# Hybrid attention, convolution and expert block on one core: four high-part buffers, full-width row operations, and one-hot masks built by two tokens

## Chip, cores and metric

The program runs on one core of one Trainium2 chip. The metric is device time in microseconds (us). Before the change three runs took 1897.51, 1898.70 and 1901.18 us, median 1898.7 us. The profile is of one further execution, which took 1894.76 us.

## What is computed

The input is 256 tokens of width 2048. A first half (adaLN modulation, differential attention, causal convolution, output projection) takes about a quarter of the time and is not touched except for the layout of its last product. The second half is an expert retrieval (PEER) over 128 x 128 experts, of which each token picks 16 for each of 8 heads:

```python
q = (h @ w_q).reshape(T, PEER_HEADS, PEER_KEY_DIM)
s1 = jnp.einsum('thd,kd->thk', qb[..., :half], k1)
s2 = jnp.einsum('thd,kd->thk', qb[..., half:], k2)
v1, i1 = lax.top_k(s1, PEER_TOPK)
v2, i2 = lax.top_k(s2, PEER_TOPK)
cand = v1[..., :, None] + v2[..., None, :]
top, pos = lax.top_k(cand, PEER_TOPK)
g = jax.nn.softmax(top)
act = jax.nn.gelu(jnp.einsum('thkd,td->thk', u_tab[idx], hb)) * g
return jnp.einsum('thk,thkd->td', act, v_tab[idx])
```

## The kernel before

**Two ways through the experts.** For 192 tokens (TD) the kernel computes the product with all 16384 rows of u densely, and later the product with all rows of v, with a routing matrix that is zero where an expert was not picked. For the last 64 tokens (TS) it gathers the picked rows: 64 gathers of 128 rows of u (one row of 2048 floats per partition), each turned into 128 dot products by DVE, and 64 gathers of v, each added to a sum by DVE.

**Units.** Weights come as 544 units of 128 x 1024 floats, two to a block of 1 MB, into a ring `raw` of eight units. To keep accuracy with the fast fp32r format each unit is split: ACT copies it to fp32r (the high part, `w_hi`, function `hi`), DVE subtracts to get the low part (`w_low`, function `lo`), and PE multiplies the high part with the activations' high and low parts (L887, 8 matmuls of 2 x 192 columns) and the low part with the high activations (L894, 8 matmuls of 192 columns). `w_hi` has two buffers: `hi` of unit s waits until PE (`hi_used`) and DVE (`lo_ready`) are done with unit s - 2.

**Stages.** WQ (32 units, all 256 tokens, L1093), then the dense product with u in three stages, UP (64 units), MID (64) and ROUTE (128), then the product with v, DOWN (256 units, L1235). A stage runs in iterations of 16 units; the first is written out, the others are a hardware loop. Within an iteration the units are numbered j = 0 to 15, and each engine has its own fixed order of work by unit:

- PE, `product`: for each block (units 2m and 2m + 1) high then low matmuls of each half. A block's low activations' share stands in another part of the PSUM bank; ACT copies it out (`put_low`, L708, after the block's last matmul), and PE adds it back with an identity matmul (`add_low`, L868). This stands at the start of the second half of the next block. Then ACT applies gelu (L716), which frees the bank for the block after the next.
- DVE in UP and MID: `lo` for each unit, between them the steps of the top-k chain (`experts`, two in 16 units). In MID and ROUTE also the dots of gathered rows (`dots_at`, L1314), each row in two halves of 1024 with a read of the accumulator behind each; MID has 4 rows in an iteration, ROUTE 6, DOWN 4 row sums (`add_row`, L1741), also in halves.
- ROUTE builds the routing matrix for 24 tokens in an iteration, in 6 groups of 4: DVE makes two one-hot masks for each token (`make_masks`: L1277 the first for four tokens at once, L1282 the second for each, scaled by the gate in the same instruction) in one buffer, PE multiplies them (`weights`, L1187, 4 matmuls fp32, two records each), ACT copies the result out (`put_weights`, L731). The tables MASK, USE and PUT say at which unit each engine does group g. The single buffer ties them: `make_masks(g)` waits for `weights(g - 1)`.
- ACT: for each unit `hi`, then `put_low` at odd and gelu at even units, then in ROUTE `put_weights` at the units of PUT.
- SP brings the weights, POOL gathers the rows: u rows into two buffers, v rows into four (`got`).

```python
USE, MASK, PUT = (1, 4, 6, 9, 12, 14), (0, 3, 5, 8, 11, 13), (3, 6, 8, 11, 14, 15)
DOTS_ROUTE_FIRST = DOTS_ROUTE = (0, 1, 3, 4, 5, 6, 8, 9, 11, 12, 13, 14)
act.wait_ge(hi_used, at(i, ph.per, s - 1))
act.wait_ge(lo_ready, at(i, ph.per, s - 1))
```

Of the kernel before, what the change touches and what calls it, by code (L numbers as in the profile page):

```python
# [92 lines left out]
SUMS_FIRST, SUMS_AT = (6, 8, 9, 10, 12, 13, 14, 15), (0, 2, 4, 6, 8, 10, 12, 14)  # L93
# [10 lines left out]
def build_block(nc, x, c, c_row, w_ada, w_gate_f, b_cols, g_cols, rows, w_front, lambdas, g_subln, conv_w,  # L104
                conv_vecs, peer_wq, peer_keys, peer_u, u_rows, peer_v, out):
    with ExitStack() as ctx:
# [88 lines left out]
        a_pair = a2[:, :].rearrange("p (k m t) -> p k m t", m=2, t=T)  # L195
        a_hi, a_lo = a_pair[:, :, 0, :], a_pair[:, :, 1, :]
# [1663 lines left out]
```

## Time and profile before

| | |
|---|---|
| median of three runs | 1898.7 us |
| profiled execution | 1894.76 us, span 1892.9 us |
| PE / PE weight load busy | 1796.9 us (95%) / 1564.3 us (83%) |
| DVE busy | 1605.2 us (85%) |
| ACT busy | 850.1 us (45%) |
| POOL busy | 181.2 us (10%) |
| HBM traffic | 617.98 MB, mean 326 GB/s |
| chain that ended last | PE 73%, DVE 13%, issue 7%, DMA 6% |

The chain follows the work that ended last back from the end; its longest piece is PE's L1235 (DOWN), 582.93 us. Busy shares are averages over stages that have different limits, so they say little of what a change in one stage is worth: a stage is read by its own windows and by the rows of one iteration.

### The profile page before, as it was taken

How to read it: one execution, taken by the hardware profiler on the slowest of the kernel's cores; microseconds unless marked ns; L12 is line 12 of the kernel's file. 1: busy time of each engine (PE TensorE's matmuls, PEld its weight loads, DVE VectorE, ACT ScalarE, POOL GpSimd, SP SyncE). 2: the span in 40 equal slices, each digit the busy share in tenths (PEclk: the TensorE clock that was granted, in tenths of full speed). 3: DMA queues.
4: the chain of work that ended last, by engine and by line, in shares of the span. 5: the costliest groups of instructions: out<-in, count | busy, mean ns of one | idle time of the engine just before them, and what ended most of it. 6: DMA issues, size and time to landing. Idle time of an engine off the chain costs nothing.

```text
span 1892.9 us, 29014 instructions
## 1 busy us (share of the span) xinstructions
PE 1796.9 (95%) x9902; PEld 1564.3 (83%) x9902; DVE 1605.2 (85%) x2621; ACT 850.1 (45%) x1208; POOL 181.2 (10%) x145
## 2 busy tenths in 40 slices
PE   4999999898899999888899999999999999999997
PEld 4888888443899999777899999997888888888885
DVE  3668898766677999999999999997988888888887
ACT  3001222300645555444456666665554555555544
POOL 1000000000000000100021221211111111111110
PEclk9999999999899999999999999999999999999999
DMA  8998556699596677977889999999999999999994
GB/s 344 418 421 334 224 222 225 256 392 422 206 346 246 225 246 248 341 284 282 290 295 362 362 362 364 351 365 351 396 363 371 369 363 375 365 365 373 366 383 183
DMA packets 96785, 617.98 MB, mean 326 GB/s; under 512 B 11697, under 2 KB 20433, under 8 KB 25041
## 3 DMA queue, kind: packets, MB, share of 16 engines
q1 hardware_dynamic: 66960, 465.60, 64.1%
q0 software_dynamic: 18496, 134.24, 18.7%
q10 hardware_dynamic: 11266, 17.32, 2.5%
q8 instruction: 38, 0.62, 0.1%
q14 instruction: 25, 0.20, 0.0%
HBM read 600.26 MB, written 16.79 MB: 326 GB/s over the span
## 4 chain that ended last, share of the span: by engine, by line
PE 73%; DVE 13%; issue 7%; DMA 6%; ACT 1%; DVEq 0%; ACTq 0%; SPq 0%
PE ps L1235 31%; PE ps L887 10%; PE ps L894 6%; PE ps L932 6%; PE ps L916 4%; PE ps L1093 4%; PE ps L1043 3%; PE ps L943 3%; DMA early<-in_w_front 2%; DVE w_low L1292 2%; PE ps L1187 2%; DVE big L1314 2%; DMA early<-in_w_ada 1%; DMA big<-in_w_gate_f 1%; DMA gsub<-in_g_subln 1%
## 5 line engine op out<-in xcount | busy, mean ns | idle before, releaser
L616 ACT ACTIVATE w_hi<-raw 128x1024 fp32r<-128x1024 f32 x544 | 577.0, 1061 | 638.9 <-PE ps L1235 245.1
L1292 DVE TENSOR_TENSOR w_low<-raw,w_hi 128x1024 fp32r<-128x1024 f32 x544 | 661.5, 1221 | 103.2 <-ACT w_hi L616 95.1
L887 PE MATMUL ps<-a,w_hi 128*128 128x384 f32 x2048 | 410.2, 341 | 4.9 <-ACT stage L716 4.0
L1235 PE MATMUL ps<-w_hi,a 128*128 128x512 f32 x1536 | 391.2, 390 | 3.8 <-DVE a L1715 3.8
L887 PEld LDWEIGHTS ps<-a,w_hi 128*128 128x128 f32 x2048 | 347.6, 189 | 5.9 <-ACT stage L716 4.1
L1235 PEld LDWEIGHTS ps<-w_hi,a 128*128 128x128 f32 x1536 | 288.9, 188 | 64.3 <-issue 4.0
L894 PEld LDWEIGHTS ps<-a,w_low 128*128 128x128 f32 x2048 | 261.7, 191 | 41.6 <-DVE w_low L1292 40.4
L894 PE MATMUL ps<-a,w_low 128*128 128x192 f32 x2048 | 270.2, 274 | 27.3 <-DVE w_low L1292 27.1
L1235 PE MATMUL ps<-w_low,a 128*128 128x512 f32 x1024 | 274.6, 390 | 0.0
L1235 PEld LDWEIGHTS ps<-w_low,a 128*128 128x128 f32 x1024 | 192.5, 188 | 40.7 <-DVE w_low L1292 0.7
L439 POOL DMA_INDIRECT big<-in_u_rows,row_ix x64 | 84.8, 1325 | 800.3 <-DVE dots_now L1314 431.5
L1314 DVE CUSTOM_DVE_ANT_0 big<-big 128x1024 f32<-128x1024 f32 x128 | 155.7, 1217 | 0.0
L1339 DVE CUSTOM_DVE_ANT_0 early<-early,big 128x2048 f32<-128x2048 f32 x32 | 72.7, 2288 | 28.1 <-DMA early<-in_w_ada 28.1
L1339 DVE CUSTOM_DVE_ANT_0 raw<-raw,big 128x2048 f32<-128x2048 f32 x32 | 73.0, 2288 | 27.6 <-DMA raw<-in_w_ada 27.6
L1395 DVE SCALAR_TENSOR_TENSOR big<-big 128x256 f32<-128x256 f32 x240 | 96.4, 477 | 0.0
L1741 DVE SCALAR_TENSOR_TENSOR big<-early,row_act,big 128x1024 f32<-128x1024 f32 x64 | 81.8, 1278 | 0.0
L1741 DVE SCALAR_TENSOR_TENSOR big<-big,row_act 128x1024 f32<-128x1024 f32 x62 | 79.3, 1278 | 0.0
L1093 PE MATMUL ps<-a,w_hi 128*128 128x256 f32 x512 | 69.4, 290 | 0.9 <-DVE a L1569 0.9
L439 POOL DMA_INDIRECT big<-in_peer_v,row_ix x32 | 44.4, 1389 | 250.1 <-DVE big L1741 206.7
L1043 PE MATMUL ps<-early,big 128*128 128x512 f32 x128 | 59.5, 619 | 7.9 <-DMA early<-in_w_front 7.9
L439 POOL DMA_INDIRECT early<-in_peer_v,row_ix x32 | 44.8, 1399 | 226.0 <-DVE big L1741 222.8
L1093 PEld LDWEIGHTS ps<-a,w_hi 128*128 128x128 f32 x512 | 65.0, 196 | 1.2 <-DVE a L1569 1.2
(228 smaller groups left out, 1818.2 us busy)
## 6 DMA issues: line engine op xcount, KB each, us to landing
raw<-in_peer_u SPq DMA_DIRECT2D x128, 1024.0 KB
raw<-in_peer_v SPq DMA_DIRECT2D x128, 1024.0 KB
raw<-in_w_ada SPq DMA_DIRECT2D x40, 1024.0 KB, 10.9
early<-in_w_ada SPq DMA_DIRECT2D x40, 1024.0 KB, 10.3
raw<-in_w_front SPq DMA_DIRECT2D x28, 1024.0 KB, 8.8
early<-in_w_front SPq DMA_DIRECT2D x28, 1024.0 KB, 9.3
raw<-in_peer_wq SPq DMA_DIRECT2D x16, 1024.0 KB
big<-in_w_gate_f SPq DMA_DIRECT2D x16, 1024.0 KB, 7.4
```

The costliest lines, as they stand in the source:

```text
L439: gp.indirect_dma_start(where, None, table, bass.IndirectOffsetOnAxis(ap=row_ix[:, n:n + 1], axis=0))\
L616: act.activation(w_hi[:, s % 2, :], raw[:, s % RING, :], ACT.Copy).then_inc(hi_ready, 1)
L887: done = pe.matmul(ps[:, b % 2, 0:2 * TD].rearrange("p (m t) -> p m t", m=2), w_hi[:, half, k * P:(k + 1) * P], a_pair[:, kc, :, 0:TD], st ...
L894: done = pe.matmul(ps[:, b % 2, 0:TD], w_low[:, s % RING, k * P:(k + 1) * P], a_hi[:, kc, 0:TD], start=False, stop=False, skip_group_check ...
L932: done = pe.matmul(ps[:, e % 2, 0:T], slots[n % SLOTS][:, kc * P:(kc + 1) * P], hT[:, kc, :], start=kc == 0, stop=kc == KC - 1)
L1043: done = pe.matmul(ps[:, (MIX_FIRST, MIX_SECOND)[half][bank], :], mixed(place)[:, tt * P:(tt + 1) * P], slots[n % SLOTS][:, cols:cols + 51 ...
L1093: return pe.matmul(ps[:, banks[blk // 2], (blk % 2) * T:(blk % 2 + 1) * T], w[:, blk * P:(blk + 1) * P], a[:, k, :], start=k == 0 and m == ...
L1235: done = pe.matmul(ps[:, 4 * tt + 2 * (j % 2) + n, :], a, w[:, n * 512:(n + 1) * 512], start=i is None and blk == 0 and m in (0, 2), stop= ...
L1292: dve.tensor_tensor(w_low[:, s % RING, :], raw[:, s % RING, :], w_hi[:, s % 2, :].bitcast(F32), ALU.subtract).then_inc(lo_ready, 1)
L1314: d = dve.tensor_tensor_reduce(got[buf][:, cols], got[buf][:, cols], h_tok[:, cols], 1.0, 0.0, ALU.mult, ALU.add, dots_now[:, n, half:half ...
L1339: dve.tensor_tensor_reduce(slots[n % SLOTS], slots[n % SLOTS], c_all, 1.0, 0.0, ALU.mult, ALU.add, macc[:, group, k:k + 1]).then_inc(mod_u ...
L1741: d = dve.scalar_tensor_tensor(acc[:, cols], got[n][:, cols], row_act[:, bass.ds(at(i, 4, n), 1)], acc[:, cols], ALU.mult, ALU.add)
```

## The change

1. **Four high-part buffers.** The activations `a2` are laid out in four quarters of 64 tokens. From UP on only 192 tokens are used, so the last quarter (2048 floats) serves as two further buffers for high parts; `hi` of unit s then waits for unit s - 4 (`high_back`). WQ still has two. PE's moving operand, which was two runs of 192 floats (or one), becomes six runs of 64 (or three).
2. **`add_low` earlier.** It moves from the start of a block's second half to between the high and the low matmuls of its first half.
3. **Full-width rows.** Dots and row sums are one instruction of 2048 in place of two of 1024, at new places. v rows use two buffers in place of four.
4. **Masks by two tokens.** 12 groups h of two tokens, in two buffers. DVE makes both masks of both tokens with one comparison of 512 elements (L1301), ACT multiplies the second by the gate (`scale_masks`, L742, two instructions of 128 x 128), PE does 2 matmuls (L1211). `make_masks(h)` waits for `weights(h - 2)`.

```diff
-USE, MASK, PUT = (1, 4, 6, 9, 12, 14), (0, 3, 5, 8, 11, 13), (3, 6, 8, 11, 14, 15)
-DOTS_MID_FIRST, DOTS_MID = tuple(range(8, 16)), (1, 2, 5, 6, 9, 10, 13, 14)
-DOTS_ROUTE_FIRST = DOTS_ROUTE = (0, 1, 3, 4, 5, 6, 8, 9, 11, 12, 13, 14)
+MASK_FIRST, USE_FIRST, PUT_FIRST = ((4, 4, 6, 6, 8, 8, 10, 10, 12, 12, 14, 14),
+                                    (5, 5, 7, 7, 9, 9, 11, 11, 13, 13, 15, 15), (7, 9, 11, 13, 15, 15))
+MASK, USE, PUT = ((0, 1, 2, 4, 5, 6, 8, 9, 10, 11, 12, 13), (1, 2, 3, 5, 6, 7, 9, 10, 11, 12, 13, 14),
+                  (4, 7, 9, 12, 14, 15))
+DOTS_MID_FIRST, DOTS_MID = (9, 11, 13, 15), (2, 6, 10, 14)
+DOTS_ROUTE_FIRST = DOTS_ROUTE = (1, 3, 6, 9, 12, 14)
-SUMS_FIRST, SUMS_AT = (6, 8, 9, 10, 12, 13, 14, 15), (0, 2, 4, 6, 8, 10, 12, 14)
+SUMS_FIRST, SUMS_AT = (8, 10, 12, 14), (1, 4, 9, 12)
...
-        a_pair = a2[:, :].rearrange("p (k m t) -> p k m t", m=2, t=T)
-        a_hi, a_lo = a_pair[:, :, 0, :], a_pair[:, :, 1, :]
+        a_quarters = a2[:, :].rearrange("p (q k m t) -> p k m q t", k=KC, m=2, t=TS)
+        a_pair = a_quarters[:, :, :, 0:TD // TS, :]
+        w_hi_more = a2[:, KC * 2 * TD:KC * 2 * T].rearrange("p (s n) -> p s n", n=UNIT)
+        highs = [w_hi[:, 0, :], w_hi[:, 1, :], w_hi_more[:, 0, :], w_hi_more[:, 1, :]]
...
+        def high(ph, j):
+            return highs[(ph.s + j) % (2 if ph is PH_WQ else 4)]
+
+        def high_back(ph, j, i):
+            return 2 if ph is PH_WQ or (ph is PH_UP and i is None and j < 2) else 4
...
+                back = high_back(ph, j, i)
                 if s >= 2 or i is not None:
-                    act.wait_ge(hi_used, at(i, ph.per, s - 1))
-                    act.wait_ge(lo_ready, at(i, ph.per, s - 1))
+                    act.wait_ge(hi_used, at(i, ph.per, s - back + 1))
+                    act.wait_ge(lo_ready, at(i, ph.per, s - back + 1))
...
+            def scale_masks(h, i):
+
+                act.wait_ge(oh_masked, at(i, 12, h + 1))
+                for t in range(2):
+                    token = bass.ds(at(i, 24, 2 * h + t), 1)
+                    done = act.activation(masks[:, h % 2, 1, t, :], masks[:, h % 2, 1, t, :], ACT.Copy,
+                                          scale=sel_T[:, 2, token])
+                done.then_inc(oh_ready, 1)
...
-                    if half and (b > B_UP or i is not None):
-                        add_low(b - 1, i, ph.blocks)
...
                     done.then_inc(hi_used, 1)
+                    if half == 0 and (b > B_UP or i is not None):
+                        add_low(b - 1, i, ph.blocks)
...
-                dve.tensor_tensor(masks[:, 0], iota[:, None, :].to_broadcast([P, 4, P]),
-                                  sel_T[:, 0, bass.ds(at(i, 24, 4 * g), 4)].unsqueeze(2).to_broadcast([P, 4, P]),
-                                  ALU.is_equal)
-                for t in range(4):
-                    token = bass.ds(at(i, 24, 4 * g + t), 1)
-                    done = dve.tensor_scalar(masks[:, 1, t, :], iota[:, :], sel_T[:, 1, token], sel_T[:, 2, token],
-                                             ALU.is_equal, ALU.mult)
-                done.then_inc(oh_ready, 1)
+                if i is not None or h >= 2:
+                    dve.wait_ge(oh_used, at(i, 12, h - 1))
+                dve.tensor_tensor(masks[:, h % 2], iota[:, None, None, :].to_broadcast([P, 2, 2, P]),
+                                  sel_T[:, 0:2, bass.ds(at(i, 24, 2 * h), 2)].unsqueeze(3).to_broadcast([P, 2, 2, P]),
+                                  ALU.is_equal).then_inc(oh_masked, 1)
...
+                dve.tensor_tensor_reduce(got[buf], got[buf], h_tok, 1.0, 0.0, ALU.mult, ALU.add, dots_now[:, n:n + 1])\
+                    .then_inc(row_used, 1)
...
+                    d = dve.scalar_tensor_tensor(acc, got[n % 2], row_act[:, bass.ds(at(i, 4, n), 1)], acc, ALU.mult,
+                                                 ALU.add)
```

How the order moves at two places. First ACT in the loop of ROUTE, from the high part of unit 4 to the copy of the low share at unit 5. Before (`w_hi<-raw` is `hi`, `stage<-ps` gelu, `low<-ps` `put_low`):

```order
L616 ACTIVATE w_hi<-raw 128x1024 [waits lo_ready,hi_used]
L713 REGISTER_ALU
L715 REGISTER_ALU [waits summed]
L716 ACTIVATE stage<-ps 128x192 [waits gel_out0]
L614 REGISTER_ALU
L616 ACTIVATE w_hi<-raw 128x1024 [waits lo_ready,hi_used]
L708 ACTIVATE low<-ps 128x192 [waits split_used]
```

And with the change, from the gelu of unit 4 on (`oh<-oh,sel_T` scales one mask, `big<-ps` is `put_weights`):

```order
L725 ACTIVATE stage<-ps 128x192 [waits gel_out0]
L739 REGISTER_ALU
L742 ISA [waits oh_masked]
L742 ACTIVATE oh<-oh,sel_T 128x128
L742 ISA
L742 ACTIVATE oh<-oh,sel_T 128x128
L749 ISA [waits oh_used]
L749 ACTIVATE big<-ps 128x4x128
L625 ACTIVATE w_hi<-raw 128x1024 [waits lo_ready,hi_used]
L716 REGISTER_ALU
L717 ACTIVATE low<-ps 128x192 [waits split_used]
```

Between the gelu of unit 4 and the high part of unit 5 there now stand a wait for DVE's mask, two scalings and a `put_weights`; the copy of the low share comes behind all of them.

Second, PE in the same loop, one block (here units 4 and 5). Before:

```order
L887 MATMUL ps<-a,w_hi 128x384 [waits hi_ready]
L887 MATMUL ps<-a,w_hi 128x384 x7
L894 MATMUL ps<-a,w_low 128x192 [waits lo_ready]
L894 MATMUL ps<-a,w_low 128x192 x7
L867 REGISTER_ALU
L868 MATMUL ps<-low,ident_r 128x192 [waits low_put]
```

With the change:

```order
L906 MATMUL ps<-a,w_hi 128x384 [waits hi_ready]
L906 MATMUL ps<-a,w_hi 128x384 x7
L888 REGISTER_ALU
L889 MATMUL ps<-low,ident_r 128x192 [waits low_put]
L915 MATMUL ps<-a,w_low 128x192 [waits lo_ready]
L915 MATMUL ps<-a,w_low 128x192 x7
```

The identity matmul, and with it PE's wait for ACT's copy (`low_put`), stands eight low matmuls earlier.

## Rows read from the trace of the kernel before

**Rows 1.** Windows: UP, one iteration of MID, ROUTE, DOWN; window, length, each engine, clock, DMA

```profile
640.00:690.00 50.00, 50.00 (x355) 50.00 (x355) 46.86 (x132) 28.12 (x43) 0.00 (x0) 1.00 0.71 236
820.89:868.11 47.22, 40.47 (x266) 36.99 (x265) 44.55 (x118) 21.65 (x32) 4.47 (x4) 1.00 0.79 283
1034.00:1077.00 43.00, 43.00 (x314) 43.00 (x313) 42.12 (x72) 26.71 (x38) 8.35 (x7) 1.00 0.94 360
1366.00:1513.00 147.00, 147.00 (x650) 121.72 (x649) 129.45 (x123) 75.00 (x73) 22.58 (x16) 1.00 0.97 369
```

**Rows 2.** Timeline, PE in ROUTE: start, length, instruction group

```profile
1123.47 0.28 PE L868 MATMUL ps<-low,ident_r 128*128 128x192 f32 x1
1123.58 1.58 PE L887 MATMUL ps<-a,w_hi 128*128 128x384 f32 x8
1125.00 1.03 PE L894 MATMUL ps<-a,w_low 128*128 128x192 f32 x8
1125.87 1.08 PE L1187 MATMUL ps<-oh 128*128 128x128 f32 x8
1126.70 1.66 PE L887 MATMUL ps<-a,w_hi 128*128 128x384 f32 x8
1128.20 1.03 PE L894 MATMUL ps<-a,w_low 128*128 128x192 f32 x8
```

**Rows 3.** Timeline, all engines, ROUTE: DVE's masks wait for PE

```profile
1147.36 1.08 PE L1187 MATMUL ps<-oh 128*128 128x128 f32 x8
...
1148.59 0.69 DVE L1277 TENSOR_TENSOR oh<-iota,sel_T 128x512 f32<-128x512 f32 x1 [0.56 <-PE ps L1187]
1149.20 1.11 DVE L1282 TENSOR_SCALAR oh<-iota,sel_T 128x128 f32<-128x128 f32 x4
...
1150.22 1.22 DVE L1292 TENSOR_TENSOR w_low<-raw,w_hi 128x1024 fp32r<-128x1024 f32 x1
```

**Rows 4.** Timeline, DVE in ROUTE, the same iteration further on

```profile
1151.36 1.22 DVE L1314 CUSTOM_DVE_ANT_0 big<-big 128x1024 f32<-128x1024 f32 x1
...
1153.64 1.22 DVE L1314 CUSTOM_DVE_ANT_0 big<-big 128x1024 f32<-128x1024 f32 x1
...
1155.13 1.26 DVE L1292 TENSOR_TENSOR w_low<-raw,w_hi 128x1024 fp32r<-128x1024 f32 x1
```

**Rows 5.** Timeline, DVE in the first half: the same operation, 2048 wide

```profile
360.65 2.28 DVE L1339 CUSTOM_DVE_ANT_0 early<-early,big 128x2048 f32<-128x2048 f32 x1
...
362.86 2.29 DVE L1339 CUSTOM_DVE_ANT_0 early<-early,big 128x2048 f32<-128x2048 f32 x1
```

**Rows 6.** Groups by form, ACT: 128 x 128 with one operand per partition

```profile
L519 ACT ACTIVATE big<-big,tiny 128x128 f32<-128x128 f32 x16 | 6.3, 392 | 21.6 <-DVE tiny L1413 21.6
```

**Rows 7.** Timeline, ACT in ROUTE: high part, low share, weights, high part

```profile
1120.50 1.06 ACT L616 ACTIVATE w_hi<-raw 128x1024 fp32r<-128x1024 f32 x1 [1.99 <-PE ps L887]
1121.47 0.31 ACT L708 ACTIVATE low<-ps 128x192 fp32r<-128x192 f32 x1
...
1122.17 1.13 ACT L731 ACTIVATE big<-ps 128x512 f32 x1 [0.39 <-issue]
1123.09 1.07 ACT L616 ACTIVATE w_hi<-raw 128x1024 fp32r<-128x1024 f32 x1
```

**Rows 8.** Timeline, all engines, from ROUTE to DOWN

```profile
1286.85 1.06 ACT L616 ACTIVATE w_hi<-raw 128x1024 fp32r<-128x1024 f32 x1 [1.29 <-DVE w_low L1292]
...
1287.81 0.31 ACT L708 ACTIVATE low<-ps 128x192 fp32r<-128x192 f32 x1
1287.94 1.27 DVE L1292 TENSOR_TENSOR w_low<-raw,w_hi 128x1024 fp32r<-128x1024 f32 x1 [1.12 <-ACT w_hi L616]
...
1288.27 0.33 PE L868 MATMUL ps<-low,ident_r 128*128 128x192 f32 x1 [0.59 <-ACT low L708]
```

**Rows 9.** DMA issues in DOWN: gathers, median us to landing

```profile
big<-in_peer_v,row_ix POOLq DMA_INDIRECT x8, 7.7
```

**Rows 10.** Chain of waits, a piece of WQ: start, length, what

```profile
488.08 2.87 PE ps L1093 x24
```

More of the change, by code:

```diff
@@ L202, in build_block @@
         slots = pairs + [early[:, n * D:(n + 1) * D] for n in range(4)]
-        got = [region(24576 + n * D, D) for n in range(2)] + [early[:, 3072 + n * D:3072 + (n + 1) * D] for n in range(2)]
+        got = [region(24576 + n * D, D) for n in range(2)]
         ones = sb("ones", [P, P])
@@ L290, in build_block @@
         row_in = [sem(f"row_in{n}") for n in range(2)]
-        v_row_in = [sem(f"v_row_in{n}") for n in range(4)]
+        v_row_in = [sem(f"v_row_in{n}") for n in range(2)]
         row_used, v_row_used, dots_put, row_gelu, row_act_made = (sem("row_used"), sem("v_row_used"), sem("dots_put"),
@@ L1104, in query_blocks @@
                 for blk in range(8):
-                    done = part(blk, w_low[:, u % RING], a_hi, 2)
+                    done = part(blk, w_low[:, u % RING], 0, 2)
                 done.then_inc(split_used, 1)
@@ L1179, in _, with weights @@
                     product(PH_MID, n, i)
-            def weights(g, i):
-                pe.wait_ge(oh_ready, at(i, 6, g + 1))
-                if i is not None:
+            def weights(h, i):
+                g = h // 2
+                pe.wait_ge(oh_ready, at(i, 12, h + 1))
+                if i is not None and h % 2 == 0:
                     pe.wait_ge(w_evac, at(i, 6, g - 5))
-                for t in range(4):
-                    done = pe.matmul(ps[:, 2 + g, t * P:(t + 1) * P], masks[:, 1, t, :], masks[:, 0, t, :], start=True,
-                                     stop=True)
+                for t in range(2):
+                    token = 2 * (h % 2) + t
+                    done = pe.matmul(ps[:, 2 + g, token * P:(token + 1) * P], masks[:, h % 2, 1, t, :],
+                                     masks[:, h % 2, 0, t, :], start=True, stop=True)
                 done.then_inc(oh_used, 1)
@@ L1227, in down @@
                     first, low, second = (a_down[:, blk, P:2 * P], a_down[:, blk, 0:P], a_down[:, blk, 2 * P:3 * P])
-                    high, lower = w_hi[:, j % 2], w_low[:, j % RING]
-                    for m, (tt, a, w) in enumerate(((0, first, high), (0, low, high), (1, second, high),
+                    upper, lower = high(PH_DOWN, j), w_low[:, j % RING]
+                    for m, (tt, a, w) in enumerate(((0, first, upper), (0, low, upper), (1, second, upper),
                                                     (0, first, lower), (1, second, lower))):
@@ L1297, in lo, with dots_at @@
                     dots_at(j, i, DOTS_ROUTE if i is not None else DOTS_ROUTE_FIRST, ROW_ROUTE, N_ROUTE)
-            def dots_at(j, i, halves, row0, per):
-                if j not in halves:
+            def dots_at(j, i, places, row0, per):
+                if j not in places:
                     return
-                n, half = halves.index(j) // 2, halves.index(j) % 2
+                n, many = places.index(j), len(places)
                 first = (0 if row0 == ROW_MID else ROW_ROUTE_FIRST) if i is None else row0 - per
-                buf, cols = (first + n) % 2, slice(half * UNIT, (half + 1) * UNIT)
-                if half == 0:
-                    dve.wait_ge(row_in[buf], at(i, 16 * per // 2, 16 * ((first + n) // 2 + 1)))
-                if n == 0 and half == 0:
+                buf = (first + n) % 2
+                dve.wait_ge(row_in[buf], at(i, 16 * per // 2, 16 * ((first + n) // 2 + 1)))
+                if n == 0:
                     if i is not None or row0 != ROW_MID:
```

102 lines of the change are left out of this document (45 added, 57 removed).

## The prediction

> **What bounds the kernel now.** I read the stage windows first, then one iteration of each stage in the timeline. In UP, ROUTE and DOWN PE is busy without a gap: 50.00 of 50 us, 43.00 of 43, 147.00 of 147, at a granted clock of 1.00 [rows 1]. In MID it is not (40.47 of 47.22), and DVE is (44.55 of 47.22; the rest are the short gaps between dependent steps of the top-k chain) [rows 1]. So DVE time is worth something in MID alone, and in the PE-bound stages a change can gain nothing on DVE or ACT, but can lose if a wait reaches PE. In ROUTE DVE is at 42.12 of 43.00, so the cover there is thin.
>
> ROUTE's 43.00 us can be counted from PE's starts [rows 2]: high matmuls 1.42 us (1123.58 to 1125.00), low ones 0.87, `add_low` 0.11, a group of four mask products 0.83, and the high group behind it takes 1.50 in place of 1.42, so a group costs 0.91. 16 x 2.29 + 8 x 0.11 + 6 x 0.91 = 42.98.
>
> **The change, part by part.**
>
> *Full-width dots.* A half dot advances DVE by 1.14 us (1150.22 to 1151.36 is the same step for `lo`, both 1.22 long) [rows 3, 4], the 2048-wide form by 2.21 (360.65 to 362.86) [rows 5]. A row saves 2 x 1.14 - 2.21 = 0.07 us. MID has 16 rows: -1.1 us on the path. Bounds: 0 from below; from above the durations (2 x 1.22 - 2.28 = 0.16) and the accumulator read that falls away, for which the 0.35 us that a read and a copy take together (1153.64 to 1155.13 less 1.14) [rows 4] leave at most 0.17: 0.33 a row, -5.3 us. I take the step from start to start, as DVE is full there. The Trainium skill (VectorE: DVE Perf Modes, the section on the TRN2 errata) says an instruction pays a fixed term of about 150 cycles once whatever its size; by that, an estimate, a row would save 0.16 us and MID 2.5. In ROUTE and DOWN the saving is under PE's cover.
>
> *Mask products in twelve groups of two.* The same 24 matmuls, but the 0.08 us behind each group comes twelve times: a group of two costs between 0.455 (half of 0.91) and 0.495 (0.415 + 0.08), I take 0.475. That is 12 x 0.475 - 5.46 = +0.24 us an iteration; the first keeps pairs together. 7 x 0.24 = +1.7 us (0 to +3.4).
>
> *Masks on DVE, scaling on ACT.* DVE loses 1.02 us per four tokens (1149.20 to 1150.22) and does the comparison twice, 0.61 each [rows 3]: 10 us become 7 in an iteration, which is under PE. ACT gets 24 scalings. The nearest row has one operand per partition, 128 x 128, 392 ns [rows 6]; successive ACT instructions overlap by about 0.09 (1.06 long, 0.97 from start to start) [rows 7], so a pair takes 0.60 us. ACT's total of 26.7 us grows by 7 and is no bound; what counts is where it stands.
>
> *Where it stands.* `hi` of unit j + 1 is now queued behind the scaling for unit j, which waits for DVE, and `put_low` of an odd unit behind that `hi`; `put_low` releases `add_low`, and PE's wait for it comes 0.87 us earlier than before. I follow the longest chain in ROUTE, from PE's products of h8 at unit 11 (time 0) to `add_low` at unit 4 of the next iteration:
> - products to DVE's next mask: four take 1.23 (1147.36 to 1148.59) [rows 3], two 1.23 - 0.415 = 0.82.
> - mask h10 0.61, `lo` 1.14, dot 2.21: 3.96.
> - mask h11 to `lo` of unit 14, by way of ACT: 0.69 mask, 0.10, pair 0.60, `hi` to `lo` 1.09 (1286.85 to 1287.94) [rows 8]: 2.48.
> - `lo`, dot, read and copy of the dots 0.35 [rows 4], `lo`, mask, `lo`, mask, `lo`, dot: 10.55.
> - mask h2 to `lo` of unit 3, again through ACT: 2.48. Then `lo` and dot: 3.35.
> - mask h3 0.69 + 0.10, pair 0.60, `put_weights` 0.92 and `hi` 0.97 [rows 7], `put_low` to `add_low` 0.46 (1287.81 to 1288.27) [rows 8]: 3.74.
>
> Sum 27.38 us. PE without a wait needs for the same way units 11 to 15 and 0 to 3 and the high matmuls of unit 4: 9 x 2.29 + 4 x 0.11 (units 12, 14, 0, 2) + 7 groups x 0.475 + 1.42 = 25.8. PE stands still for 1.6 us in each iteration, and after it DVE has slack again until unit 11. The loop has seven passes: 7 x 1.6 = **+11.2 us**. Each of some 20 steps is good to a few hundredths, the pair and `put_weights` to 0.2; I give the wait 0.7 to 2.6 us.
>
> *Four buffers.* In MID DVE is full and gains nothing by having high parts earlier; in UP and DOWN PE is full. At the passage from ROUTE to DOWN DVE waits 1.12 us for ACT's second high part [rows 8], ahead of work that PE waits for; ACT's own row of steps follows close. I take -0.7 (0 to -1.1).
>
> *v rows in two buffers.* In DOWN a row is used at units 1, 4, 9, 12; from one use of a buffer to its next are 8 units of 2.27 us less the add's own 2.3, some 15.9 us, for 7.7 from issue to landing [rows 9]: 0. All transfers share DMA engines that are 0.97 busy [rows 1], so this is the cover to watch. u rows in ROUTE have 5 units, 11.2 us.
>
> *Moving operand in runs of 64.* Cost taken as 0; it is a rival below.
>
> Sum: -1.1 + 1.7 + 11.2 - 0.7 = +11.1. Against the profiled execution 1894.8 + 11.1 = 1905.9; the median of the runs is 3.9 above that execution, so for the median 1898.7 + 11.1 = **1910 us**.
>
> **Rivals.**
>
> *Covered.* The chain is 1.6 us shorter than I count, of 27, and PE never waits. For it: PE never waits in ROUTE now, and DVE's sum in an iteration is only 12 x 0.61 + 16 x 1.14 + 6 x 2.21 + 0.35 = 39.2 us. Against it: the waits through ACT, which no such sum holds. Time 1898.7 - 1.1 + 1.7 - 0.7 = 1898.6: no change.
>
> *Faster.* Covered too, and a row in MID saves 0.25 us (-4.0), the passage gives its whole 1.1, and a mask group of two costs just half: -5.1, 1893.6. It decides from 0.17 us a row on. For it: MID's period of 47.22 is all DVE. Against: the measured step of 2.21.
>
> *Runs cost.* PE's 384 columns now come in two runs and take 1.42 / 8 = 0.1775 us [rows 2], 0.0175 over 384 columns at 2.4 GHz; 256 in one run take 2.87 / 24 = 0.1196 [rows 10], 0.013 over. If the difference, 0.004, is the price of a run, four more cost 0.016 on each of 8 matmuls in the 192 units of UP and ROUTE: +25 us; ROUTE's wait is then covered, so 1898.7 + 25 - 1.8 = 1922. The Trainium skill (SBUF — State Buffer, the section on the DMA port swizzle) says that accesses within a 16-byte line run at full bandwidth; runs of 64 floats keep to that, so by it this rival costs nothing. No run here shows it yet.
>
> *Late gathers.* If landings in DOWN reach 17 us, each row costs PE the excess: +1 us x 64. Small chance.
>
> **Numbers.** A measurement of this kernel can tell about 0.2%, 3.8 us, from no change. Chances: the forecast 0.54, covered 0.20, faster 0.16, runs cost 0.07, late gathers 0.03. The forecast's own range, with 0.7 to 2.6 us of wait, is 1903.5 to 1917; both bounds of the other terms widen it by 3. To leave out no more than 2 in 10 the range takes in covered and faster: 1893 to 1920. Slower by over 0.2%: 0.54 + 0.07 + 0.03 = 0.64; within: 0.20; faster: 0.16.
>
> **What would show it.** Right: in ROUTE a period of 44.8 us in place of 43.0, and at unit 4 of each iteration PE's identity matmul (L889) waiting some 1.6 us for ACT (L717), with DVE's `lo` (L1311) waiting for `hi` (L625) after masks h2 and h11. MID's period 46.9. UP and DOWN (2.27 us a unit) as before. A scaling of 0.39 us. Wrong: PE dense in ROUTE (then covered), eight high matmuls in UP taking more than 1.42 (runs cost), DVE's sums in DOWN waiting for DMA (late gathers), MID at 46.2 or less (faster).

## The result, and the profile after

| | before | after |
|---|---|---|
| median | 1898.5 us (6 runs, 1894.6 to 1901.2) | 1912.5 us (6 runs, 1907.3 to 1912.8) |
| profiled execution, span | 1894.76, 1892.9 us | 1912.49, 1910.7 us |

The ratio is 1.0069, 95% interval 1.0054 to 1.0084: slower, by over three times what a measurement of this kernel can tell. The forecast was 1910.

The page of the changed kernel, busy time by engine and the chain that ended last:

```profile
PE 1803.7 (94%) x9902; PEld 1571.3 (82%) x9902; DVE 1574.3 (82%) x2285; ACT 876.1 (46%) x1400; POOL 193.9 (10%) x145
...
PE 71%; DVE 12%; issue 7%; DMA 7%; ACT 1%; DVEq 0%; ACTq 0%; SPq 0%
```

DVE works 31 us less than before (1605.2 to 1574.3) and the kernel takes 18 us more: where PE sets the time, less work on DVE gains nothing. The same four windows as [rows 1], of the changed kernel:

```profile
640.00:690.00 50.00, 50.00 (x353) 50.00 (x353) 46.75 (x129) 28.06 (x44) 0.00 (x0) 1.00 0.70 239
797.88:844.79 46.91, 41.31 (x261) 39.55 (x260) 44.24 (x110) 20.09 (x32) 4.46 (x4) 0.93 0.79 289
1087.30:1132.28 44.98, 43.68 (x313) 42.89 (x313) 39.64 (x42) 32.28 (x63) 7.20 (x6) 1.00 0.91 344
1366.00:1513.00 147.00, 147.00 (x650) 121.76 (x649) 127.83 (x106) 70.94 (x73) 26.38 (x17) 1.00 0.96 368
```

UP is as it was, an iteration of MID takes 46.91 us (47.22), one of ROUTE 44.98 (43.00), and in ROUTE PE has idle time for the first time. DOWN's middle is dense as before. The waits in ROUTE (950 to 1302 us), in total, times and longest, name what PE lacks:

```profile
ACT oh L742 <- DVE oh L1301: 91.3, 67, 2.8
DVE oh L1301 <- PE ps L1211: 20.9, 23, 1.7
...
PE ps L889 <- ACT low L717: 9.7, 8, 1.3
```

The 91 us that ACT waits are free by themselves, but its `hi` and `put_low` stand behind them. The chain of the prediction, in the timeline, from PE's products of h8 at unit 11 to `add_low` at unit 4 of the next iteration:

```profile
1104.75 0.63 PE L1211 MATMUL ps<-oh 128*128 128x128 f32 x4
...
1105.53 0.69 DVE L1301 TENSOR_TENSOR oh<-iota,sel_T 128x512 f32<-128x512 f32 x1 [1.04 <-PE ps L1211]
...
1107.27 2.29 DVE L1332 CUSTOM_DVE_ANT_0 big<-big 128x2048 f32<-128x2048 f32 x1
...
1111.98 1.23 DVE L1311 TENSOR_TENSOR w_low<-raw,a 128x1024 fp32r<-128x1024 f32 x1 [0.68 <-ACT a L625]
...
1122.81 0.69 DVE L1301 TENSOR_TENSOR oh<-iota,sel_T 128x512 f32<-128x512 f32 x1
...
1125.32 1.22 DVE L1311 TENSOR_TENSOR w_low<-raw,a 128x1024 fp32r<-128x1024 f32 x1 [0.68 <-ACT a L625]
...
1128.67 0.69 DVE L1301 TENSOR_TENSOR oh<-iota,sel_T 128x512 f32<-128x512 f32 x1
...
1129.38 1.59 PE L906 MATMUL ps<-a,w_hi 128*128 128x384 f32 x8
1129.49 0.69 ACT L742 ACTIVATE oh<-oh,sel_T 128x128 f32<-128x128 f32 x2 [2.83 <-DVE oh L1301]
1130.09 1.07 ACT L749 ACTIVATE big<-ps 128x512 f32 x1
...
1130.96 1.05 ACT L625 ACTIVATE w_hi<-raw 128x1024 fp32r<-128x1024 f32 x1
1131.91 0.31 ACT L717 ACTIVATE low<-ps 128x192 fp32r<-128x192 f32 x1
...
1132.28 0.35 PE L889 MATMUL ps<-low,ident_r 128*128 128x192 f32 x1 [1.30 <-ACT low L717]
```

It reads from top to bottom as one string: DVE's mask waits for PE, `lo` waits for ACT's `hi` after masks h11 and h2 (0.68 us each), mask h3 ends, and ACT then does two scalings, `put_weights`, `hi` and `put_low` before PE may add. PE finished its high matmuls 1.3 us earlier. The wait comes in all seven passes of the loop, at 997.34, 1042.32, 1087.30, 1132.28 and so on.

**Where the 17.8 us between the two spans went.** Start times of the same work in both traces, up to ACT's `hi` of unit 4 in ROUTE's first iteration (it waits there for the transfer `row_gate<-big`): before 949.50, after 945.83, so -3.7. From there to DOWN's first matmul (1292.42, 1302.80): 342.9 and 357.0, +14.1. DOWN itself, to the first matmul behind it (1875.19, 1892.95): 582.8 and 590.2, +7.4. The tail takes 17.7 us in both. The prediction had -1.1, +12.2 and 0. The medians differ by 14.0 us and not by 17.8, since the profiled execution of the kernel before was 3.8 us faster than its median.

DOWN's +7.4 is not a pace. A unit still takes 2.27 us; there is one wait of 0.76 us at 1354 and one long stop near the end, where the group that should start at 1867.98 starts at 1873.15. The timeline of the changed kernel there (SP and POOL issue, ACT and PE wait):

```profile
1850.40 0.43 SPq L383 DMA_DIRECT2D big<-x_saved  x1
...
1850.88 0.43 SPq L384 DMA_DIRECT2D big<-gate_saved  x1
...
1852.01 1.68 POOL L449 DMA_INDIRECT big<-in_peer_v,row_ix  x1 [9.38 <-DVE big L1754]
...
1854.57 13.93 SPq L333 DMA_DIRECT2D raw<-in_peer_v  x4
...
1859.58 1.41 POOL L449 DMA_INDIRECT big<-in_peer_v,row_ix  x1 [5.90 <-DVE big L1754]
...
1872.04 2.00 ACT L625 ACTIVATE w_hi<-raw 128x1024 fp32r<-128x1024 f32 x2 [9.08 <-DMA raw<-in_peer_v]
...
1873.15 2.93 PE L1259 MATMUL ps<-w_hi,a 128*128 128x512 f32 x6 [5.01 <-ACT w_hi L625]
```

The chain that ended last says the same: `DMA raw<-in_peer_v` holds it for 17.45 us from 1854.57. Before, the last gather was issued at 1835.81, ahead of the two loads at 1839.37 and 1839.84:

```profile
1835.81 1.15 POOL L439 DMA_INDIRECT early<-in_peer_v,row_ix  x1 [8.11 <-DVE big L1741]
...
1839.37 0.43 SPq L373 DMA_DIRECT2D big<-x_saved  x1
...
1839.84 0.43 SPq L374 DMA_DIRECT2D big<-gate_saved  x1
...
1843.53 13.93 SPq L323 DMA_DIRECT2D raw<-in_peer_v  x4
...
1855.77 2.01 ACT L616 ACTIVATE w_hi<-raw 128x1024 fp32r<-128x1024 f32 x2 [3.00 <-DMA raw<-in_peer_v]
```

There ACT waited 3.00 us for the weight, and PE not at all. Two buffers let a gather start only when the row two places earlier has been added, so two gathers of 1 MB fall behind the issue of the 3 MB that the tail needs. The weight behind them landed 17.45 us after its issue (1854.57 to 1872.02), before 12.2 us (1843.53 to 1855.77); the difference of 5.2 us is about what 2 MB take at the 414 to 425 GB/s of that stretch (5 us, an estimate).

### The profile page after: what moved, and what is told of

The parts are those of the page before. It is cut to its first block, busy times and chain, and to the rows that moved or that the text cites. A ratio compares the mean times of both kernels' runs of the same rounds, so it can differ in the third digit from the quotient of the medians.

```text
span 1910.7 us, 29072 instructions
## 1 busy us (share of the span) xinstructions
PE 1803.7 (94%) x9902; PEld 1571.3 (82%) x9902; DVE 1574.3 (82%) x2285; ACT 876.1 (46%) x1400; POOL 193.9 (10%) x145
## 4 chain that ended last, share of the span: by engine, by line
PE 71%; DVE 12%; issue 7%; DMA 7%; ACT 1%; DVEq 0%; ACTq 0%; SPq 0%
PE ps L1259 29%; PE ps L906 9%; PE ps L915 6%; PE ps L953 6%; PE ps L937 4%; PE ps L1114 4%; PE ps L1064 3%; PE ps L964 3%; DMA early<-in_w_front 3%; PE ps L1211 2%; DVE big L1332 2%; DVE w_low L1311 2%; DMA raw<-in_peer_v 1%; DMA early<-in_w_ada 1%; DMA gsub<-in_g_subln 1%
## 5 line engine op out<-in xcount | busy, mean ns | idle before, releaser
L1311 DVE TENSOR_TENSOR w_low<-raw,w_hi 128x1024 fp32r<-128x1024 f32 x288 | 349.2, 1222 | 75.9 <-ACT w_hi L625 71.5
L625 ACT ACTIVATE w_hi<-raw 128x1024 fp32r<-128x1024 f32 x288 | 298.9, 1056 | 233.9 <-DMA raw<-in_peer_v 77.5
L1311 DVE TENSOR_TENSOR w_low<-raw,a 128x1024 fp32r<-128x1024 f32 x256 | 310.2, 1222 | 55.8 <-ACT a L625 52.3
L625 ACT ACTIVATE a<-raw 128x1024 fp32r<-128x1024 f32 x256 | 264.3, 1052 | 92.0 <-DMA raw<-in_peer_v 75.5
L906 PE MATMUL ps<-a,w_hi 128*128 128x384 f32 x1024 | 208.8, 346 | 4.4 <-ACT stage L725 3.6
L906 PE MATMUL ps<-a 128*128 128x384 f32 x1024 | 208.0, 344 | 0.0
L1259 PE MATMUL ps<-w_hi,a 128*128 128x512 f32 x768 | 197.6, 393 | 8.6 <-ACT w_hi L625 5.0
L1259 PE MATMUL ps<-a 128*128 128x512 f32 x768 | 194.9, 389 | 0.0
L906 PEld LDWEIGHTS ps<-a,w_hi 128*128 128x128 f32 x1024 | 176.2, 191 | 4.9 <-ACT stage L725 3.7
L906 PEld LDWEIGHTS ps<-a 128*128 128x128 f32 x1024 | 175.0, 190 | 0.5 <-issue 0.5
L1259 PEld LDWEIGHTS ps<-a 128*128 128x128 f32 x768 | 144.2, 188 | 29.9
L742 ACT ACTIVATE oh<-oh,sel_T 128x128 f32<-128x128 f32 x192 | 66.1, 395 | 91.3 <-DVE oh L1301 91.3
```

Source lines behind the costliest of these rows:

```text
L625: act.activation(high(ph, j), raw[:, s % RING, :], ACT.Copy).then_inc(hi_ready, 1)
L742: done = act.activation(masks[:, h % 2, 1, t, :], masks[:, h % 2, 1, t, :], ACT.Copy, scale=sel_T[:, 2, token])
L906: done = pe.matmul(ps[:, b % 2, 0:2 * TD].rearrange("p (m q t) -> p m q t", m=2, t=TS), high(ph, 2 * n + half)[:, k * P:(k + 1) * P], a_pa ...
L1259: done = pe.matmul(ps[:, 4 * tt + 2 * (j % 2) + n, :], a, w[:, n * 512:(n + 1) * 512], start=i is None and blk == 0 and m in (0, 2), stop= ...
L1311: dve.tensor_tensor(w_low[:, s % RING, :], raw[:, s % RING, :], high(ph, j).bitcast(F32), ALU.subtract).then_inc(lo_ready, 1)
```

## Experiments

Theory A: ROUTE loses by the chain through ACT. Theory C: DOWN loses by the last gathers meeting the tail's loads. The letters in the expectations are these and their rivals. Medians are of 4 to 12 runs, each with its ratio to runs of the kernel before on the same chip.

**low_back: `add_low` back where it was.**

```diff
+                    if half and (b > B_UP or i is not None):
+                        add_low(b - 1, i, ph.blocks)
                     if ahead:
                         ahead(2 * n + half, i)
...
-                    if half == 0 and (b > B_UP or i is not None):
-                        add_low(b - 1, i, ph.blocks)
```

> The changed kernel with add_low back at the start of a block's second half; all else as changed. Theory A (PE's 1.3 us at L889 in unit 4 of each ROUTE iteration is the end of the chain through ACT, whose length doesn't hang on where add_low stands): PE now comes 0.87 us later to add_low, so the wait is about 0.45 us, ROUTE's period 44.1 in place of 44.97, and the kernel 7 x 0.87 = 6 us faster than the changed one, about 1906.5 us. Rival B (the loss of ROUTE is spread: twelve product groups and runs of 64 cost PE time, the wait is only where it shows): the period stays within 0.2 us of 44.97 and the time near 1912.

Measured: 1905.2 us, ratio 1.0042 (1.0027 to 1.0058). PE in ROUTE:

```profile
1083.42 0.36 PE L889 MATMUL ps<-low,ident_r 128*128 128x192 f32 x1 [0.60 <-ACT low L717]
...
1127.53 0.36 PE L889 MATMUL ps<-low,ident_r 128*128 128x192 f32 x1 [0.59 <-ACT low L717]
```

The two starts are 44.11 us apart, where 44.1 was expected: PE came 0.87 us later to a wait that stays where it was in time, and got that much back. Theory A holds; B, the spread loss, doesn't.

**put_at_5: the weights' copy behind the low share.**

```diff
-                  (4, 7, 9, 12, 14, 15))
+                  (5, 7, 9, 12, 14, 15))
```

> The changed kernel with put_weights of the first group at unit 5 in place of 4, so behind put_low of unit 5 and not ahead of it. Theory A: the chain to add_low at unit 4 loses put_weights' 0.9 us; wait 0.4 us, period 44.1, time 6 us under the changed kernel, 1906.5 us. Rival B2 (ACT isn't what is late, DVE's masks are, and ACT would only wait longer for them): the copy that PE waits for starts no earlier, period 44.97, time 1912.

Measured: 1905.4 us, ratio 1.0041 (1.0026 to 1.0057). The same place:

```profile
1083.73 0.36 PE L889 MATMUL ps<-low,ident_r 128*128 128x192 f32 x1 [0.44 <-ACT low L717]
...
1127.83 0.36 PE L889 MATMUL ps<-low,ident_r 128*128 128x192 f32 x1 [0.43 <-ACT low L717]
```

Period 44.10. One ACT instruction of 0.9 us, moved behind one of 0.3, is worth 6 us of ROUTE in this kernel (7 x 0.88). So it is ACT's own queue, and not only DVE's mask, that is late.

**masks_by_four: the masks as before.** All functions of the mask groups are those of the kernel before, with its tables, in the otherwise changed kernel:

```diff
-                act.wait_ge(oh_masked, at(i, 12, h + 1))
...
-                    done = act.activation(masks[:, h % 2, 1, t, :], masks[:, h % 2, 1, t, :], ACT.Copy,
-                                          scale=sel_T[:, 2, token])
...
+                    done = dve.tensor_scalar(masks[:, 1, t, :], iota[:, :], sel_T[:, 1, token], sel_T[:, 2, token],
+                                             ALU.is_equal, ALU.mult)
```

> The changed kernel with the masks as before (groups of four, one buffer, scaled on DVE, the old tables), so no scaling on ACT; four high buffers, early add_low, full-width rows and two v buffers as changed. Theory A (all of ROUTE's loss comes with the chain through ACT): PE without a wait over 0.3 us in ROUTE's loop, period 43.0 to 43.3 in place of 44.97; the time falls by 12 to 14 us to about 1899. Rival B (early add_low or runs of 64 cost in ROUTE): period 43.8 or more, 1904 or more. Rival G (DVE, with 1.02 us for each of 24 scalings of four more, is late for the low parts): PE waits for DVE, not ACT.

Measured: 1899.0 us, ratio 1.0003 (0.9991 to 1.0014). ROUTE's period is 43.00 in six of the seven passes. In one (1109.65 to 1154.45) it is 44.80: DVE waited 1.44 us for a gathered u row (1108.78), and PE, whose row shows 0.44 us at 1112.66, lost 1.8 in that pass. Whether the full-width dots made that row late isn't shown; in four_mended, which has them too, no pass is longer. Otherwise early `add_low`, full-width dots and runs of 64 cost nothing in ROUTE once no scaling stands in ACT's queue; the mask scheme (groups, places and scaling, which this run changes together) carries all of ROUTE's loss. Its profiled execution, at 1905.2 the slowest of ten, has two stops elsewhere: 4.81 us at the end of DOWN, and before DOWN this:

```profile
1292.56 0.96 DVE L1709 TENSOR_TENSOR big<-big,oh 128x768 f32<-128x768 f32 x1 [5.26 <-DMA oh<-gel_saved]
```

**before_two_v2: the kernel before with two v buffers.**

```diff
-                elif n < 4:
-                    gp.wait_ge(split_used, PH_DOWN.s)
                 else:
-                    gp.wait_ge(v_row_used, n - 3)
-                gather(n, v_rows, got[n % 4], v_row_in[n % 4])
+                    gp.wait_ge(v_row_used, n - 1)
+                gather(n, v_rows, got[n % 2], v_row_in[n % 2])
```

> The kernel before with v rows in two buffers; nothing else changed, sums still in halves at the old places. Theory C (two buffers move the last gathers into the loads of x_saved and gate_saved): PE dense through ROUTE and most of DOWN as before, and one stop of 2.5 to 5 us behind 1840; DOWN 586 to 590 us in place of 582.8; time 3 to 6 us over the kernel before, 1902 to 1905. Rival D (the stop needs the full-width sums or four high buffers): no stop, 1898.6.

Measured: 1905.4 us, ratio 1.0046 (1.0029 to 1.0062). PE in DOWN, and DVE ahead of PE's first stop:

```profile
1338.38 1.28 DVE L1739 SCALAR_TENSOR_TENSOR big<-big,row_act 128x1024 f32<-128x1024 f32 x1 [3.02 <-DMA big<-in_peer_v,row_ix]
...
1339.58 2.35 DVE L1290 TENSOR_TENSOR w_low<-raw,w_hi 128x1024 fp32r<-128x1024 f32 x2
...
1340.85 2.07 PE L1233 MATMUL ps<-w_low,a 128*128 128x512 f32 x4 [2.88 <-DVE w_low L1290]
...
1867.33 1.67 PE L1233 MATMUL ps<-w_hi,a 128*128 128x512 f32 x6 [2.33 <-ACT w_hi L614]
```

The stop near the end is there with nothing else changed, at 2.33 us, the low end of what was expected; DOWN takes 590.0 us (1295.82 to 1885.77), just over its upper end. A second stop at its beginning, 2.88 us, was not expected. Theory C holds for the stop at the end. The one at the beginning is the two buffers' as well, but by another way: DVE's sum waits 3.02 us for a gathered row, `lo` stands behind the sum, and PE waits for `lo`. That gather was issued at 1328.89, when the sums had freed its buffer, and landed 9.5 us later. Other kernels have a stop there too, from other causes (see *Open*). The passage from ROUTE to DOWN is longer as well (PE waits 6.12 us, before 3.83); whether that is the buffers' doing isn't shown.

**tail_loads_late: the tail's loads after unit 11.**

```diff
-                if j == 7:
+                if j == 11:
                     sp.wait_ge(at_lo, GROUPS // 2)
```

> The changed kernel with x_saved and gate_saved loaded after unit 11 of the last iteration in place of unit 7. Theory C: the two loads (3 MB) no longer meet the last two gathers and the weight that PE lacked; PE's stop at the end shrinks from 5.0 to under 1 us; the final sum may wait for x_saved for 0 to 3 us instead, so 2 to 5 us faster, 1907.5 to 1910.5. Rival D: the stop stays at 5 us, time 1912 or more.

Measured: 1908.9 us, ratio 1.0061 (1.0037 to 1.0085). DOWN takes 586.3 us (1301.77 to 1888.06) in place of 590.2, and the stop is halved, not gone:

```profile
1877.22 1.73 PE L1259 MATMUL ps<-w_hi,a 128*128 128x512 f32 x6 [2.33 <-ACT w_hi L625]
```

The size of the stop proves little here: put_at_5, with the loads at the old place, has 2.62 us, and by the ratios (1.0061 and 1.0069) this kernel and the changed one can't be told apart. What the trace does show is that both gathers are now issued ahead of the loads (1848.93 and 1854.60, loads at 1857.16) and a stop remains: weights still follow the two loads on SP's queue, and PE needs them sooner. The tail was no longer than before.

**four_v_rows: four v buffers, for two high parts in DOWN.**

```diff
-            return highs[(ph.s + j) % (2 if ph is PH_WQ else 4)]
+            return highs[(ph.s + j) % (2 if ph in (PH_WQ, PH_DOWN) else 4)]
...
-                gather(n, v_rows, got[n % 2], v_row_in[n % 2])
+                gather(n, v_rows, got[n % 4], v_row_in[n % 4])
```

> The changed kernel with v rows in four buffers again; for that, high parts in DOWN have two buffers. Rows still full width at units 1, 4, 9, 12. Theory C (PE's 5.0 us stop at 1868 comes from gathers that are still under way when x_saved and gate_saved load in the last iteration, since two buffers put each gather two rows nearer to its use): no stop of more than 1 us near the end, DOWN 583 to 585 us long in place of 590.2, time 5 to 7 us under the changed kernel, 1906 us. Rival D (full-width sums or the four high buffers themselves disturb DOWN): the stop stays, DOWN 588 or more, and 1912; two high buffers might then even add waits of PE for ACT.

Measured: 1912.0 us, ratio 1.0082 (1.0058 to 1.0105). The stop at the end is gone, as C wants, but the time is not: DOWN takes 589.2 us (1302.59 to 1891.77). The timeline shows a loss that comes twice in 16 units, where DVE builds a share of the matrix (L1723) just behind a full-width sum (L1756):

```profile
1497.26 2.35 DVE L1756 SCALAR_TENSOR_TENSOR big<-big,row_act 128x2048 f32<-128x2048 f32 x1
...
1499.52 0.95 DVE L1723 TENSOR_TENSOR big<-big,stage 128x768 f32 x1
...
1500.26 1.52 PE L1261 MATMUL ps<-w_hi,a 128*128 128x512 f32 x6
...
1501.67 1.19 PE L1261 MATMUL ps<-w_low,a 128*128 128x512 f32 x4
1502.46 1.23 DVE L1313 TENSOR_TENSOR w_low<-raw,w_hi 128x1024 fp32r<-128x1024 f32 x1 [0.84 <-ACT w_hi L627]
...
1502.69 1.55 PE L1261 MATMUL ps<-w_hi,a 128*128 128x512 f32 x6
```

PE's unit is 2.43 us long here (1500.26 to 1502.69), not 2.27, and PE's row names no wait. With two high buffers ACT's next `hi` waits for DVE's late `lo`, and DVE then for `hi`. The experiment swapped one cover for another, so it can't price the v buffers alone; before_two_v2 does.

**two_high_bufs: two high-part buffers throughout.**

```diff
-            return highs[(ph.s + j) % (2 if ph is PH_WQ else 4)]
+            return highs[(ph.s + j) % 2]
...
-            return 2 if ph is PH_WQ or (ph is PH_UP and i is None and j < 2) else 4
+            return 2
```

> The changed kernel with two high-part buffers in all stages. Theory E (the four buffers do earn time, which the prediction put at next to nothing: DVE enters MID ahead, and in DOWN they cover the full-width sums): UP and MID up to ROUTE's first hi 2 to 3 us later than in the changed kernel, each unit of DOWN behind which DVE builds a share of the matrix 0.17 us longer (as in the run with four v rows), so DOWN +5 us; ROUTE the same or worse; in all +7 to +13 us: 1919 to 1925. Rival F (the gains ahead of ROUTE come from the full-width dots alone, and the slow pace of DOWN in the run with four v rows from its v rows in other memory): 1912, no more than 1 us ahead of ROUTE.

Measured: 1914.5 us, ratio 1.0085 (1.0068 to 1.0102): 2 us behind the changed kernel, or 3 by the ratios, not 7 to 13; the two intervals overlap, so the runs alone don't show that it is slower. In the traces two terms of theory E are seen. In DOWN the unit of 2.43 us comes once in eight (1504.18 less 1501.74 is 2.44), so 32 x 0.18 = 6 us. The v rows lie where they lie in the changed kernel, so rival F's other memory isn't the reason. And in UP's first iteration DVE waits for `hi` with two buffers. DVE's timeline there, in the kernel before:

```profile
613.25 1.23 DVE L1292 TENSOR_TENSOR w_low<-raw,w_hi 128x1024 fp32r<-128x1024 f32 x1 [1.73 <-ACT w_hi L616]
```

In this one:

```profile
611.32 1.22 DVE L1311 TENSOR_TENSOR w_low<-raw,w_hi 128x1024 fp32r<-128x1024 f32 x1 [1.71 <-ACT w_hi L625]
```

In the changed kernel the same `lo` waits for nothing:

```profile
611.00 1.23 DVE L1311 TENSOR_TENSOR w_low<-raw,w_hi 128x1024 fp32r<-128x1024 f32 x1
```

From the `lo` two units ahead of that (607.12, 605.20 and 606.56 us) to the end of PE's stop at unit 4 of ROUTE's first iteration (the high group there starts at 950.82, 946.87 and 947.15) it is 343.7 us in the kernel before, 341.7 with two buffers and 340.6 with four: four buffers are worth 1.1 us up to there, once. Against that the stop at the end of DOWN was 1.82 us for 5.01, and DOWN took 593.7 us in place of 590.2, 3.5 more and not 6. A slower PE leaves the transfers more time, which would explain the shorter stop but wasn't tried by itself. So E is right in its places and too high in its total.

**mended_three, mended_again, four_mended.** The first two are one kernel: both edits in ROUTE, and the tail's loads behind the last weights.

```diff
-                if j == 7:
+                if j == 15:
                     sp.wait_ge(at_lo, GROUPS // 2)
```

> The changed kernel with three edits: add_low back at the second half, put_weights of the first group at unit 5, and x_saved and gate_saved loaded behind the last weights (unit 15). Theory A: the waits of 0.60 and 0.45 us that are left with one edit each vanish; period 43.1 to 43.4. Theory C: no stop of PE at the end of DOWN, the last sum may wait 0 to 3 us for x_saved. Together 1912.5 - 12 - 5 + 0 to 3 = 1895.5 to 1899. Rivals: a second chain holds the period at 43.8 or more (B); the stop only moves behind PE's end and costs the same 5 us there (H): then 1901 or more.

Measured: 1893.4 us, ratio 0.9992 (0.9979 to 1.0005). ROUTE's period is 43.26, no row names a wait of PE in its loop, DOWN takes 583.3 us (1289.09 to 1872.41) with no stop behind 1341, and the tail is 17.7 us as ever: rival H falls, the loads have time enough behind the weights. Once more, in eleven runs:

> The kernel of mended_three once more, to settle against the kernel before: its ten runs had a median of 1893.4 us against 1897.6, but one of 1901 and an interval of 0.9979 to 1.0005. By the two profiles it should be 2 to 4 us faster: ROUTE 43.26 in place of 43.00 (7 x 0.26 = +1.8), UP and MID to ROUTE's start -3, DOWN 583.3 in place of 582.8, passage -0.3 to -1. Ratio 0.998 to 0.999. Rival: the median was luck and the ratio is 1.000 or more.

Measured: 1893.9 us, ratio 0.9996 (0.9986 to 1.0006). The profile's difference of -2 to -4 us isn't in the ratio: this kernel and the one before can't be told apart.

four_mended is masks_by_four with the two other edits:

> The kernel of masks_by_four with add_low back at the second half and x_saved and gate_saved loaded behind the last weights: four high buffers, full-width rows and two v buffers on top of the masks of the kernel before. Theories A and C: ROUTE's period 43.0 (1.8 us less than mended_three in seven passes), no stop at the end of DOWN (4.8 us in masks_by_four): 1891 to 1894, ratio 0.997 to 0.998. Rival: the passage to DOWN, where DVE waited 5.3 us for a load of saved gelu values in masks_by_four, is late again and takes 4 us back: 1895 to 1898.

Measured: 1893.2 us (12 runs), ratio 0.9986 (0.9974 to 0.9998). ROUTE's period is 43.00. PE's two waits at the passage to DOWN, the last ones over 0.21 us in its timeline:

```profile
1284.93 0.33 PE L874 MATMUL ps<-low,ident_r 128*128 128x192 f32 x1 [0.51 <-ACT low L714]
...
1288.45 2.90 PE L1242 MATMUL ps<-w_hi,a 128*128 128x512 f32 x6 [3.19 <-DVE a L1718]
```

Of what was run this kernel has the lowest ratio, ahead of the one before by about 0.14%, which is under the 0.2% that I take for a difference but with an interval that leaves out 1 and overlaps those of mended_three and mended_again. By the profiles its lead is made ahead of ROUTE, where the four high buffers and the full-width dots gain: from the `lo` at 605.34 to ACT's `hi` at 945.52 it is 340.2 us, before 342.4 (607.12 to 949.50), though 0.5 of the difference is the landing of `row_gate<-big` (7.51 for 7.98 us). ROUTE with the passage (342.9 us) is as before, DOWN 0.4 us shorter. The new mask scheme is not in it.

## Why the prediction was right, and where it was not

- **The chain through ACT** was right in place, steps and size. From PE's products of h8 to `add_low` the trace has 1132.28 - 1104.75 = 27.53 us, the sum said 27.38. The pair of scalings takes 0.60 (0.60 taken), `put_weights` to `hi` 0.87 (0.92), `hi` to `put_low` 0.95 (0.97), `put_low` to `add_low` 0.37 (0.46). The 1.6 us forecast was counted from start to start; so counted it is 1.47, and 1.57 with what `add_low` itself then takes (0.19 in place of 0.09): 2.90 from the high group to `add_low` (1129.38 to 1132.28), where a block without a wait takes 1.43 (1118.26 to 1119.69). The row shows 1.30 of idle time. Of the steps not named here the largest miss is DVE's stretch from `lo` of unit 14 (1111.98) to mask h2 (1122.81): 10.83 for 10.55.
- **Groups of two** were costed at +0.24 us an iteration. A group takes 0.385 and the high group behind it 1.495 in place of 1.42 (from 1120.78 to 1121.17, and 1123.51 to 1123.90 for the first): 0.46, near the bound of half a group of four; 12 x 0.46 - 5.46 = +0.06. What made up for it are small delays of `add_low` at units 0 and 2 by the same queue, 0.11 and 0.25 us (1123.90 to 1125.55 is 1.65 us, where behind a group 1.50 is usual). The period came to 44.98 for 44.8 forecast, ROUTE and passage to +14.1 for +12.2.
- **Full-width dots**: 0.31 us in 4 rows, 0.078 a row for 0.07; MID's period 46.91 for 46.9. By the fixed term of the Trainium skill (VectorE: DVE Perf Modes, the section on the TRN2 errata) the estimate was 0.16 a row. The lengths of single instructions agree with it (2 x 1.22 - 2.28 = 0.16), the steps from start to start, which set the time, don't: half of it shows. *Faster* fell with that.
- **Four buffers** were put at 0 ahead of ROUTE. That step failed: "in UP and DOWN PE is full", but in UP's first iteration DVE waited 1.73 us for `hi`, and it carries what it gains there to the end of MID: 1.1 us. In DOWN they are worth nothing over the kernel before, but without them the full-width sums cost 6 us. The passage gave 0.25 (3.83 to 3.58) for 0.7.
- **Up to ROUTE's unit 4** the change gained 3.7 us for 1.1: 1.25 dots in MID, 1.1 buffers, 0.6 that the profiled execution was ahead already at 607 us (two_high_bufs was 1.9 ahead there, so that point moves from one execution to the next), and 0.5 that the `row_gate<-big` transfers, for which ACT's `hi` of unit 4 waits, took from issue to that `hi`: 7.46 us (938.37 to 945.83), before 7.98 (941.52 to 949.50). Some 0.3 is left.
- **v rows in two buffers** were costed at 0: the step that was most wrong, in two ways. I compared the landing (7.7 us) with the time between uses in the loop (15.9) and asked if the row would be late. In the later iterations it never was. But in DOWN's first iteration the sums stand at units 8, 10, 12 and 14, so a buffer's uses are four units apart, 9.1 us less the sum's 2.3, which is less than a landing. There the changed kernel's DVE waited 1.15 us for a row (1333.95), which PE didn't feel, and before_two_v2's, with its sums in halves at other units, waited 3.02 just behind that iteration, which cost PE a stop of 2.88. The greater harm went to a third party: weights that share the DMA engines with the rows, in the one iteration in which SP brings 3 MB more. The gathers there took 10.2 us to land (median of three). The price is a stop of 1.8 to 5.0 us in the six kernels with two v buffers and the loads at the old place; the single edit in before_two_v2, with both stops and the longer passage, cost 0.46%, some 9 us. "All transfers share DMA engines" stood in the prediction as what to watch, but its rival *late gathers* looked for the loss at every row, and not at the two ends of DOWN.
- **Runs cost**: eight high matmuls in UP take 1.41 us (740.89 to 742.30), as before (1.42). Six runs of 64 floats cost nothing; by the Trainium skill's SBUF — State Buffer page (the section on the DMA port swizzle) they shouldn't, and the trace agrees.

The total of +11.1 was near the measured +14.0, but between the two profiles it is +17.8: up to ROUTE's unit 4 the change gave 2.6 more than the sum, ROUTE and the passage took 1.9 more, DOWN 7.4 more. That the medians differ by 3.8 us less than the profiled executions brought the number nearer still. The side and the main cause were right by their own working; that the number fell so near is partly luck, misses of opposite sign.

**Open.** PE has a wait of 0.2 to 2.9 us at DOWN's beginning (1339 to 1354) in eight of the eleven traces of the changed kernel and the experiments, and these name three causes. In before_two_v2 it is the late row. In the two kernels with two high buffers in DOWN it is DVE's own queue: a full-width sum and two steps of the matrix stand ahead of `lo` (from 1338.28 on in two_high_bufs), and PE waits 1.42 us in both, with two v buffers and with four. In the changed kernel, low_back and put_at_5 it is a block of weights that landed late; ACT waited 4.6 to 5.4 us for it, and PE 0.35 to 0.76. The 0.2 us of mended_three and four_mended aren't traced. Why the block landed late, and why the passage ahead of DOWN takes PE 3.2 to 7.9 us (7.9 when DVE waits 5.26 for `oh<-gel_saved`), was not tried. Whether these make the spread of 8 us among runs of one kernel isn't shown: the two profiles of the kernel of mended_three differ by 1.1 us, and there the passage is 3.59 and 3.71 us and the wait 0.19 and none.

## What to carry to other kernels

When an in-order engine gets a new link (DVE makes, ACT scales, PE uses), add up the whole cycle from start to start through every queue it passes, and compare it with the bound engine's own time for the same stretch; sums of busy time (DVE 39.6 and ACT 32.3 of 45.0 us) show slack on every engine and still miss it. If it is too long, look for an instruction that can trade places with a shorter one: one table entry gave back 6 of 14 us. And when a buffer is given up, check two things: the shortest distance between two uses of a buffer, which here was in the first iteration and not in the loop, and where its later transfers now fall. List what else the DMA queues carry in that stretch, above all in the last iteration, and put loads that only the end needs behind those that the bound engine needs.

## What the hardware showed that I had not expected

A stop costs PE more than its row says: 0.60 us of idle time at `add_low` in low_back moved the next start by 0.87 us against a block without a wait (its low group starts at 1081.68 and `add_low` at 1083.42, 1.74 us later; a low group alone takes 0.87). The 5.01 us stop in DOWN was followed by a low clock: from 1873.15 to 1875.88 the granted clock was 0.50, the 1.2 GHz level, and the six high matmuls took 2.73 us from start to start where 1.36 is usual. With the next group (1.16 for 0.91) that is 1.6 us more than the idle time, so the stop cost some 6.8 us, and not 5. The wait at 1354, counted the same way, cost 1.1; DOWN's +7.4 is 0.5 less than the two, and where that came back isn't traced.

In MID the granted clock was 0.93 in the iteration shown and 1.00 before. It fell in two stretches, each behind a wait of PE for DVE: 0.61 from 814 to 818 behind a wait of 1.59 us, 0.59 from 838 to 842 behind one of 1.89; a wait of 1.65 us at 802.41 had no such stretch behind it. The next iteration (844.79 to 891.70) ran at 1.00. That PE was busy for 41.31 us in the iteration shown, in place of 40.47, is what the lower clock makes of the same work, and in the next iteration it was 40.21. MID lost nothing by it, as DVE sets its period.
